# First slab's split in two, rotary remainders after the first evictions, memory scores ahead of the mixer's output, middle sums a tile later

## The chip, the cores and the metric

The kernel runs on one core of one Trainium2 chip. Its time is the device time of one launch in microseconds (us); of several runs the median stands. Engines: PE (TensorE: matmuls and their weight loads), DVE (VectorE), ACT (ScalarE), POOL (GpSimd) and SP, which here only issues transfers. They run side by side and meet at semaphores.

## The reference, cut to what matters

Four transformer layers at float32, on 512 tokens of width 1024. Of the first block:

```python
for l in range(DEPTH):
    h = rms_norm(x, mix_norm[l])
    kv = mem_n @ w_mem_kv[l]
    if kind == 0:
        mixed, mq = attn_mixer(h, positions, attn_w_in[j], attn_sinks[j])   # rotary, windowed heads
    else:
        mixed, mq = lru_mixer(h, lru_w_in[j], ...)        # conv, two gated recurrences, gelu gate
    mo = memory_attention(mq, mk, mv)                     # 4 heads over 256 memory tokens
    x = x + jnp.concatenate([mixed, mo], axis=-1) @ w_out[l]
    x = x + squared_relu_mlp(rms_norm(x, mlp_norm[l]), w_up[l], w_down[l])
return rms_norm(x, final_norm)
```

The second block starts from that normed output and has two layers of gated MLP (silu(h @ wg) * (h @ wu)), neighbourhood attention with gated linear attention, and a second gated MLP; a last rms norm ends it.

## The kernel before

**Layout.** Activations are held transposed: a tile is 128 features by 512 tokens, `x` has eight. Weights come in **slabs** of 128 x 2048 floats (16 blocks of 128 x 128), two buffers deep (`w_raw`, `w_hi`, `w_lo`, slot = slab number modulo 2). SP loads a raw slab when the slab two before it is split (`lo_done`). ACT then writes `w_hi`, the weights rounded to the matmul's type (`split_high`, L1332), and DVE writes the remainder `w_lo` = `w_raw` - `w_hi` (`split_low`, L1732, counted by `lo_done`). Activations are split the same way (`xg_hi`, `xg_lo`; `hid_hi`, `hid_lo`; `mixL_hi`, `mixL_lo`). Each product is three matmuls of 128 x 512: hi by hi, hi by lo, lo by hi, summed in PSUM. Eight feature tiles make 24 matmuls for one output tile, 48 for a slab of two. DVE evicts (`proj`, `tmp`, `x`), multiplying with the reciprocal root of the mean square, `r_bc`; the semaphore `evac` counts evictions, `mm_done` the matmuls of finished blocks.

**Order.** There is no scheduler: each engine's program is written out by hand and runs in that order, and semaphores alone tie them. A late instruction holds up all behind it on its engine.

**The start.** ACT splits `x` tiles 0 to 3, then the first slab as a whole, then tiles 4 to 7 and the second slab; DVE follows with the remainders. PE's first matmul waits for `lo_done` 1, the whole of the first slab. After the first slab PE sums squares over partitions (`token_rms`, L801): it waits for DVE's sum `x_sq` (L2389) and raises `ss_mm`, which releases ACT's root (`r_bc`, L1397) and POOL's squares of the memory (`mem_sq`, L638 and L641). DVE makes the rotary tables' arguments in a chain of small operations, each waiting for the one before: `rope_ang`, then for the sine (n = 0) `rope_k` three times and `rope_r` four times, then the reciprocal of `r_bc` (L1834), the eviction of slab 0 (L1772), the split of slab 2, and the chain again for the cosine (n = 1). PE, one tile into slab 1, turns values (`values()`, L1079), for which both tiles of slab 0 have to be evicted. ACT's sine (L1422) waits for both arguments, and PE's rotary swaps (L1091) for the eviction of slab 1.

**out1_0**, the first output projection (8 slabs of 12 blocks, one output tile each). Its first two slabs are multiplied in pieces inside the attention (`first_out`, L889). DVE and ACT then go slab by slab (`each_slab`): eviction into `x`, ACT `xg_hi` of the new tile, then the split of the slab two on. PE's next slab (L857) waits for that split. POOL sums squares of each new `x` tile (L655 to L661).

**The mixer of layer 1** (`mixer()` on PE, ACT and DVE). Ten slabs come in (`dense(j)` on PE, `inward(j)` on DVE, L2064), and eight recurrences run on DVE beside them (`recur`, `output`, `low`), with tanh, exp and root on ACT. Tiles 16 to 19 of `proj` (slabs 8 and 9) are the memory queries. Then the output projection: `out(h, part, b)`, 12 matmuls each (L1173), h the half of the output tiles, part 0 and 1 the mixer's features, part 2 the memory's. Memory attention has 8 units (`M1`, two heads by 128 queries): PE `scores` (L937), DVE `front` (copy, maximum, negation: L1903, L1906, L1921), ACT `exponentials` (L1431), PE `turn_probs` (L948), ACT `take_turned` (L1442), PE `weigh` (L958), DVE `back` (L1932, L1935), PE `turn_out` (L970), DVE `finish` (L1962, L1964). PE's `turn_out` of a unit waits for `finish` of the one before it. Before: PE does `out(0, 0, 0..3)`, then `scores` of units 0 and 1, then the units' loop with `out(0, 1, b)` in it.

**The middle norm.** The first block's final norm and the second block's first norm are folded together. POOL makes two sums of squares, tile by tile (`two_squares`, L675 to L689), and `token_rms` turns them over partitions with three fp32 matmuls (L804 to L806), after the first output tile of `up2_0_0_0`. Each slab there (swiglu) has two tiles, gate and up; DVE evicts both (L1804), multiplies, splits, and only then follows the split of the slab two on.

## Time and profile before

| | us |
|---|---|
| median of 3 runs | 3400.54 |
| lowest, highest | 3397.35, 3403.29 |
| the profiled execution | 3402.28 |
| its span, first to last instruction | 3400.5 |
| busy in it: PE, DVE, ACT, POOL | 3284.3, 1787.6, 1130.6, 408.6 |

Mean granted TensorE clock of the profiled execution: 0.979. The profile shows one execution; all its times are from the span's start. PE is the engine that is nearly always busy, so what the others do matters where PE waits for it, and there alone. PE's waits are the view to begin with, then the order in time around each.

### The profile page before, as it was taken

How to read it: one execution, taken by the hardware profiler on the slowest of the kernel's cores; microseconds unless marked ns; L12 is line 12 of the kernel's file. 1: busy time of each engine (PE TensorE's matmuls, PEld its weight loads, DVE VectorE, ACT ScalarE, POOL GpSimd, SP SyncE). 2: the span in 40 equal slices, each digit the busy share in tenths (PEclk: the TensorE clock that was granted, in tenths of full speed). 3: DMA queues.
4: the chain of work that ended last, by engine and by line, in shares of the span. 5: the costliest groups of instructions: out<-in, count | busy, mean ns of one | idle time of the engine just before them, and what ended most of it. 6: DMA issues, size and time to landing. Idle time of an engine off the chain costs nothing. (4 is left out here: it accounts for less than half of the span.)

```text
span 3400.5 us, 40741 instructions
## 1 busy us (share of the span) xinstructions
PE 3284.3 (97%) x15310; PEld 2700.3 (79%) x15310; DVE 1787.6 (53%) x1923; ACT 1130.6 (33%) x1314; POOL 408.6 (12%) x319
## 2 busy tenths in 40 slices
PE   7999999999899999999999899999999999799998
PEld 5887888877788887888877688888888878688887
DVE  7764534459553445434556654345444546644344
ACT  3353322259332222322333233223322334333221
POOL 1001100110100033000222420002000211520002
PEclk9999999999999999999999899999999999699999
DMA  3111222222122224232221022324222221022222
GB/s 145 63 52 61 99 99 99 109 96 81 50 99 99 87 98 117 90 108 85 100 75 62 1 87 89 108 85 129 93 102 94 104 75 63 13 74 88 102 90 79
DMA packets 46196, 293.19 MB, mean 86 GB/s; under 512 B 5424, under 2 KB 5936, under 8 KB 17936
## 3 DMA queue, kind: packets, MB, share of 16 engines
q1 hardware_dynamic: 44640, 287.04, 24.0%
q0 software_dynamic: 1456, 4.79, 0.8%
q8 instruction: 67, 1.10, 0.1%
q14 instruction: 33, 0.27, 0.0%
HBM read 289.70 MB, written 2.10 MB: 86 GB/s over the span
## 5 line engine op out<-in xcount | busy, mean ns | idle before, releaser
L1732 DVE TENSOR_TENSOR w_lo<-w_raw,w_hi 128x2048 fp32r<-128x2048 f32 (+1 forms) x288 | 677.6, 2353 | 271.1 <-ACT w_hi L1332 271.1
L857 PE MATMUL ps<-xg_hi,w_hi 128*128 128x512 f32 x1920 | 749.6, 390 | 0.0
L857 PE MATMUL ps<-xg_hi,w_lo 128*128 128x512 f32 x1920 | 747.0, 389 | 0.0
L857 PE MATMUL ps<-xg_lo,w_hi 128*128 128x512 f32 x1920 | 747.0, 389 | 0.0
L1332 ACT ACTIVATE w_hi<-w_raw 128x2048 fp32r<-128x2048 f32 (+1 forms) x288 | 544.9, 1892 | 522.5 <-PE ps L857 357.7
L857 PE MATMUL ps<-hid_hi,w_hi 128*128 128x512 f32 x1216 | 473.3, 389 | 0.0
L857 PE MATMUL ps<-hid_hi,w_lo 128*128 128x512 f32 x1216 | 473.1, 389 | 0.0
L857 PE MATMUL ps<-hid_lo,w_hi 128*128 128x512 f32 x1216 | 473.1, 389 | 0.0
L857 PEld LDWEIGHTS ps<-xg_hi,w_hi 128*128 128x128 f32 x1920 | 360.6, 188 | 76.1 <-issue 1.7
L857 PEld LDWEIGHTS ps<-xg_lo,w_hi 128*128 128x128 f32 x1920 | 360.5, 188 | 76.3 <-issue 1.6
L857 PEld LDWEIGHTS ps<-xg_hi,w_lo 128*128 128x128 f32 x1920 | 360.5, 188 | 74.9
L1817 DVE SCALAR_TENSOR_TENSOR x<-ps,x 128x512 f32 (+1 forms) x120 | 83.0, 692 | 402.1 <-PE ps L857 398.9
L1804 DVE TENSOR_TENSOR tmp<-ps,r_bc 128x512 f32<-128x512 f32 x176 | 121.7, 691 | 322.9 <-PE ps L857 307.2
L857 PEld LDWEIGHTS ps<-hid_hi,w_hi 128*128 128x128 f32 x1216 | 228.3, 188 | 48.5 <-issue 1.4
L857 PEld LDWEIGHTS ps<-hid_lo,w_hi 128*128 128x128 f32 x1216 | 228.3, 188 | 47.4
L857 PEld LDWEIGHTS ps<-hid_hi,w_lo 128*128 128x128 f32 x1216 | 228.3, 188 | 47.2
L655 POOL TENSOR_TENSOR ssq<-x 128x512 f32<-128x512 f32 x9 | 9.4, 1041 | 2047.2 <-DVE x L1817 1849.7
L1375 ACT ACTIVATE hid_hi<-tmp 128x512 f32 x88 | 55.7, 632 | 387.2 <-DVE tmp L1807 387.2
L1385 ACT ACTIVATE xg_hi<-x,vec x64 | 46.3, 724 | 350.0 <-DVE x L1817 350.0
L1000 PE MATMUL ps<-xg_hi,w_hi 128*128 128x512 f32 x384 | 154.2, 402 | 0.0
L1000 PE MATMUL ps<-xg_lo,w_hi 128*128 128x512 f32 x384 | 150.2, 391 | 0.0
L1000 PE MATMUL ps<-xg_hi,w_lo 128*128 128x512 f32 x384 | 150.1, 391 | 0.0
(337 smaller groups left out, 4103.8 us busy)
## 6 DMA issues: line engine op xcount, KB each, us to landing
w_raw<-up_dram SPq DMA_DIRECT2D x120, 1024.0 KB, 4.8
w_raw<-down_dram SPq DMA_DIRECT2D x32, 1024.0 KB, 4.8
w_raw<-down_dram SPq DMA_DIRECT2D x32, 768.0 KB, 4.3
w_raw<-down_dram SPq DMA_DIRECT2D x32, 640.0 KB, 3.8
w_raw<-in_dram SPq DMA_DIRECT2D x18, 1024.0 KB, 4.8
w_raw<-out_dram SPq DMA_DIRECT2D x14, 1024.0 KB, 4.8
w_raw<-in2n_dram SPq DMA_DIRECT2D x12, 1024.0 KB, 4.8
w_raw<-in2g_dram SPq DMA_DIRECT2D x12, 1024.0 KB, 4.8
```

The source lines that it names most:

```text
L655: pool.tensor_tensor(ssq[:], x[:, 0, :], x[:, 0, :], ALU.mult).then_inc(ssq_ready, 1)
L857: last = pe.matmul(to, (w_hi, w_lo)[wp][:, q, t:t + P], parts[xp], start=(k == 0 and m == 0), stop=(k == p.ktiles - 1 and m == 2))
L1000: last = pe.matmul(ps[:, bank, :], (w_hi, w_lo)[wp][:, s % 2, t:t + P], (xg_hi, xg_lo)[xp][:, k, :], start=(k == 0 and m == 0), stop=(k == ...
L1332: act.activation(w_hi[:, q, 0:w], w_raw[:, q, 0:w], ACT.Copy).then_inc(hi_done, 1)
L1375: act.activation(pick(hid_hi, j), tmp[:, 1, :], ACT.Copy).then_inc(hid_h, 1)
L1385: act.activation(pick(xg_hi, m), pick(x, m), ACT.Copy, scale=g).then_inc(xg_h, 1)
L1732: dve.tensor_tensor(w_lo[:, q, 0:w], w_raw[:, q, 0:w], w_hi[:, q, 0:w].bitcast(F32), ALU.subtract)\
L1804: dve.tensor_tensor(tmp[:, b, :], ps[:, 2 * q + b, :], r_bc[:], ALU.mult).then_inc(evac, Q // 2)
L1817: dve.scalar_tensor_tensor(out=pick(x, m), in0=ps[:, bank + b, :], scalar=p.alpha, in1=pick(x, m), op0=ALU.mult, op1=ALU.add).then_inc(eva ...
```

## The change

Same arithmetic, same matmuls, same transfers. Six edits, at five places in time:

1. **Start.** ACT and DVE split the first slab in two halves (one output tile each); new semaphores `first_hi` and `first_lo` tell of the first half. PE waits for `first_lo` before tile 0, for `lo_done` 1 before tile 1.
2. **Rotary chain.** The sine's remainder steps (`rope_r` for n = 0, four operations) move from before the reciprocal to after the eviction of slab 0 and the split of slab 2.
3. **out1_0.** For its first slab ACT and DVE split slab `s0 + 2` ahead of `xg_hi` and `xg_lo`, and 1536 wide instead of 2048. ACT's first iteration is written out instead of looped.
4. **Mixer, order.** PE does `scores` of unit 0 before `out(0, 0, 0)`, and of unit 1 between b = 2 and b = 3. DVE evicts the last slab before `output(6)` instead of after, and does `front` of unit 0 there. ACT's order follows.
5. **Mixer, splits.** The split of slab `MIX_O + 1` goes behind DVE's `output(7)`; that of `MIX_O + 2` from before the units into the loop, behind `back` of unit 1 (on ACT behind `take_turned` of unit 1).
6. **Middle norm.** `token_rms` comes after both tiles of the first slab of `up2_0_0_0` instead of after the first.

```diff
@@ PE, product() @@
-                slab(0, 0, (lambda: token_rms(rms)) if rms is not None else None)
+                if p.norm == MID + 1 and rms is not None:
+                    slab(0, 0)
+                    token_rms(rms)
+                else:
+                    slab(0, 0, (lambda: token_rms(rms)) if rms is not None else None)
                 slab(0, 1)
@@ PE, first_projection() @@
-                pe.wait_ge(lo_done, j + 1)
+                if j:
+                    pe.wait_ge(lo_done, j + 1)
...
                 for b in range(2):
+                    if j == 0:
+                        pe.wait_ge((first_lo, lo_done)[b], 1)
@@ PE, mixer() @@
+            pe.wait_ge(gate_read, DT)
+            pe.wait_ge(evac, EV0 + Q * (MIX_O - 1))
+            scores(M1[0])
             pe.wait_ge(evac, EV0 + Q * MIX_O)
             for b in range(4):
                 out(0, 0, b)
-            pe.wait_ge(gate_read, DT)
-            scores(M1[0])
-            scores(M1[1])
+                if b == 2:
+                    scores(M1[1])
@@ ACT, each_slab() @@
                 for q in range(2):
+                    ahead = p.name == "out1_0" and isinstance(i, int) and i == q == 0
+                    if ahead:
+                        split_high(s0 + 2, 0, p.tiles * P)
                     epilogue(i, q)
-                    if split:
+                    if split and not ahead:
@@ ACT, mixer() @@
             for n in range(DT):
+                if n + 1 == DT:
+                    gelu_square(n)
                 split(MIX_IN + n + 4)
                 if n + 1 < DT:
                     gates(n + 1, True)
                 else:
-                    gelu_square(n)
+                    exponentials(M1[0], 0)
...
-            split(MIX_O + 2)
-            exponentials(M1[0], 0)
             for n, u in enumerate(M1):
                 if n + 1 < len(M1):
                     exponentials(M1[n + 1], n + 1)
                 take_turned(u, n)
+                if n == 1:
+                    split(MIX_O + 2)
@@ ACT, start @@
-            split_high(q, q, SLAB_T * P)
+            if q == 0:
+                act.wait_ge(slab_in[0], 16)
+                for n, done in enumerate((first_hi, hi_done)):
+                    h = slice(DT * P * n, DT * P * (n + 1))
+                    act.activation(w_hi[:, 0, h], w_raw[:, 0, h], ACT.Copy).then_inc(done, 1)
+            else:
+                split_high(q, q, SLAB_T * P)
@@ DVE, resid() @@
                                              op0=ALU.mult, op1=ALU.add).then_inc(evac, Q // p.blocks)
+                if p.name == "out1_0" and isinstance(i, int) and i == q == 0:
+                    split_low(s0 + 2, 0, p.tiles * P)
@@ DVE, first_tables(); before the first eviction only rope_angles() and rope_turns(0) are left @@
             if slab == 0:
-                rope_tables(1)
+                rope_remainder(0)
+                rope_turns(1)
+                rope_remainder(1)
@@ DVE, mixer() @@
-                inward(n + 2)
-                split(MIX_IN + n + 4)
                 if n + 1 < DT:
+                    inward(n + 2)
+                    split(MIX_IN + n + 4)
                     inputs(n + 1)
+                else:
+                    front(M1[0], 0)
...
+                if n + 2 == DT:
+                    inward(DT + 1)
                 output(n)
+            split(MIX_O + 1)
             low(DT - 1)
-            split(MIX_O + 2)
-            front(M1[0], 0)
             front(M1[1], 1)
             for n, u in enumerate(M1):
                 if n + 2 < len(M1):
                     front(M1[n + 2], n + 2)
                 back(u)
+                if n == 1:
+                    split(MIX_O + 2)
                 if n:
                     finish(M1[n - 1])
```

DVE around the first eviction, in the kernel before:

```order
L2001 TENSOR_SCALAR rope_k<-rope_ang 128x512 [waits rope_step]
L2002 TENSOR_SCALAR rope_k<-rope_k 128x512 [waits rope_step]
L2003 TENSOR_SCALAR rope_k<-rope_k 128x512 [waits rope_step]
L2004 SCALAR_TENSOR_TENSOR rope_r<-rope_k,rope_ang 128x512 [waits rope_step]
L2007 SCALAR_TENSOR_TENSOR rope_r<-rope_k,rope_r 128x512 [waits rope_step] x2
L2010 TENSOR_SCALAR rope_r<-rope_r 128x512 [waits rope_step]
L1834 RECIPROCAL r_bc<-r_bc 128x512 [waits ss_rt]
L1772 TENSOR_TENSOR proj<-ps,r_bc 128x512 [waits mm_done,r_ready]
L1772 TENSOR_TENSOR proj<-ps,r_bc 128x512 [waits mm_done]
L1732 TENSOR_TENSOR w_lo<-w_raw,w_hi 128x2048 [waits hi_done]
L2001 TENSOR_SCALAR rope_k<-rope_ang 128x512
```

and with the change:

```order
L2023 TENSOR_SCALAR rope_k<-rope_ang 128x512 [waits rope_step]
L2024 TENSOR_SCALAR rope_k<-rope_k 128x512 [waits rope_step]
L2025 TENSOR_SCALAR rope_k<-rope_k 128x512 [waits rope_step]
L1858 RECIPROCAL r_bc<-r_bc 128x512 [waits ss_rt,rope_step]
L1794 TENSOR_TENSOR proj<-ps,r_bc 128x512 [waits mm_done,r_ready]
L1794 TENSOR_TENSOR proj<-ps,r_bc 128x512 [waits mm_done]
L1754 TENSOR_TENSOR w_lo<-w_raw,w_hi 128x2048 [waits hi_done]
L2033 SCALAR_TENSOR_TENSOR rope_r<-rope_k,rope_ang 128x512
L2036 SCALAR_TENSOR_TENSOR rope_r<-rope_k,rope_r 128x512 [waits rope_step] x2
L2039 TENSOR_SCALAR rope_r<-rope_r 128x512 [waits rope_step]
L2023 TENSOR_SCALAR rope_k<-rope_ang 128x512
```

The four `rope_r` operations now stand behind the reciprocal, the two evictions and the split.

DVE at the end of the mixer's recurrences, before:

```order
L2126 TENSOR_TENSOR l_v<-l_v 128x512 [waits h_done]
L2110 SCALAR_TENSOR_TENSOR l_y<-l_y,proj 128x512 [waits gelu_done]
L2130 SCALAR_TENSOR_TENSOR l_y<-l_y,l_v 128x512 [waits hs_done,gg_done]
L2064 TENSOR_TENSOR proj<-ps,r_bc 128x512 [waits mm_done] x2
L1732 TENSOR_TENSOR w_lo<-w_raw,w_hi 128x2048 [waits hi_done]
L2135 TENSOR_TENSOR mixL_lo<-l_y,mixL_hi 128x512 [waits y_hi]
L2104 SCALAR_TENSOR_TENSOR l_y<-l_y,proj 128x512 [waits gelu_step]
...
L2135 TENSOR_TENSOR mixL_lo<-l_y,mixL_hi 128x512 [waits y_hi]
L1732 TENSOR_TENSOR w_lo<-w_raw,w_hi 128x2048 [waits hi_done]
L1903 TENSOR_SCALAR sc_m<-ps 128x512 [waits s_ready]
L1906 TENSOR_REDUCE mx<-sc_m 128x2 [waits s_read]
L1921 TENSOR_SCALAR nmx<-mx 128x2 [waits mx_done]
```

and with the change:

```order
L2093 TENSOR_TENSOR proj<-ps,r_bc 128x512 [waits mm_done] x2
L2155 TENSOR_TENSOR l_v<-l_v 128x512 [waits h_done]
L2139 SCALAR_TENSOR_TENSOR l_y<-l_y,proj 128x512 [waits gelu_done]
L2159 SCALAR_TENSOR_TENSOR l_y<-l_y,l_v 128x512 [waits hs_done,gg_done]
L1929 TENSOR_SCALAR sc_m<-ps 128x512 [waits s_ready]
L1932 TENSOR_REDUCE mx<-sc_m 128x2 [waits s_read]
L1947 TENSOR_SCALAR nmx<-mx 128x2 [waits mx_done]
L2164 TENSOR_TENSOR mixL_lo<-l_y,mixL_hi 128x512 [waits y_hi]
L2133 SCALAR_TENSOR_TENSOR l_y<-l_y,proj 128x512 [waits gelu_step]
```

The eviction of the last slab (`proj`) and the first unit's scores (`sc_m`) move forward, and the split of `MIX_O + 1` leaves this place. It follows `output(7)`, and the split of `MIX_O + 2` comes to stand in the units' loop, ahead of the first unit's `finish`:

```order
L1947 TENSOR_SCALAR nmx<-mx 128x2 [waits exp_done,mx_done]
L1958 RECIPROCAL rec<-rowsum 128x2 [waits exp_done]
L1961 TENSOR_TENSOR tmp<-ps,rec 128x256 [waits o_psum,rec_done]
L1754 TENSOR_TENSOR w_lo<-w_raw,w_hi 128x2048 [waits hi_done]
L1988 CAST mixM_hi<-ps 128x2x128 [waits ot_psum]
L1990 TENSOR_TENSOR mixM_lo<-ps,mixM_hi 128x2x128 [waits ot_hi]
```

## Rows read from the trace of the kernel before

**Rows 1.** The page, busy us, share of the span and instructions of each engine.
```profile
PE 3284.3 (97%) x15310; PEld 2700.3 (79%) x15310; DVE 1787.6 (53%) x1923; ACT 1130.6 (33%) x1314; POOL 408.6 (12%) x319
```

**Rows 2.** PE's waits: line waiting <- what ended it: us in total, times, longest.
```profile
PE ps L1109 <- DVE w_lo L1732: 14.7, 1, 14.7
PE ps L1079 <- DVE proj L1772: 6.4, 1, 6.4
...
PE ps L937 <- DVE sc_m L1903: 4.1, 1, 4.1
...
PE ps L804 <- POOL tmp L689: 3.6, 1, 3.6
PE ps L1173 <- DVE proj L2064: 3.3, 1, 3.3
PE ps L857 <- DVE w_lo L1732: 3.3, 1, 3.3
```

**Rows 3.** Timeline of DVE from the start: start us, us taken, operation, count, [idle before].
```profile
12.35 2.29 DVE L1732 TENSOR_TENSOR w_lo<-w_raw,w_hi 128x2048 fp32r<-128x2048 f32 x1 [0.90 <-ACT w_hi L1332]
...
20.76 4.35 DVE L2389 TENSOR_TENSOR x_sq<-x_sq 128x2048 f32<-128x2048 f32 x3 [1.27 <-ACT x_sq L1689]
...
26.93 0.43 DVE L2003 TENSOR_SCALAR rope_k<-rope_k 128x512 f32<-128x512 f32 x1
...
28.12 4.70 DVE L2007 SCALAR_TENSOR_TENSOR rope_r<-rope_k,rope_r 128x512 f32<-128x512 f32 x2
32.85 2.47 DVE L2010 TENSOR_SCALAR rope_r<-rope_r 128x512 f32<-128x512 f32 x1
35.24 3.34 DVE L1834 RECIPROCAL r_bc<-r_bc 128x512 f32<-128x512 f32 x1
38.67 1.29 DVE L1772 TENSOR_TENSOR proj<-ps,r_bc 128x512 f32<-128x512 f32 x2
```

**Rows 4.** Timeline of POOL from 25 to 45 us.
```profile
28.30 3.97 POOL L638 TENSOR_TENSOR mem_sq<-mem_raw 128x2048 f32<-128x2048 f32 x1 [27.46 <-PE ps L801]
32.35 4.90 POOL L641 TENSOR_TENSOR mem_sq<-mem_sq 128x1024 f32<-128x1024 f32 x3
```

**Rows 5.** Stretches: us; busy (x) of PE, PEld, DVE, ACT, POOL; PEclk; DMA share, GB/s.
```profile
14.70:17.80 3.10, 3.06 (x7) 2.48 (x8) 3.10 (x5) 3.10 (x5) 0.00 (x0) 1.00 1.06 391
17.80:27.10 9.30, 9.30 (x42) 7.64 (x41) 7.75 (x9) 4.21 (x7) 0.00 (x0) 1.00 0.51 195
38.30:45.10 6.80, 4.99 (x16) 4.34 (x17) 6.54 (x10) 0.00 (x0) 0.00 (x0) 0.50 0.24 73
850.70:857.50 6.80, 5.51 (x13) 4.35 (x14) 5.50 (x7) 4.86 (x5) 0.00 (x0) 0.50 0.09 22
1311.40:1314.90 3.50, 3.50 (x6) 1.35 (x4) 0.00 (x0) 0.00 (x0) 0.00 (x0) 0.51 0.32 136
```

**Rows 6.** Timeline of PE, the token sums and the turned values.
```profile
27.19 1.02 PE L801 MATMUL ps<-x_sq,ones 128*128 128x512 f32 x2
...
40.11 1.94 PE L1079 MATMUL ps<-ident,proj 128*128 128x128 f32 x8 [6.41 <-DVE proj L1772]
```

**Rows 7.** Timeline of POOL and ACT at the first slab of out1_0.
```profile
307.98 1.04 POOL L655 TENSOR_TENSOR ssq<-x 128x512 f32<-128x512 f32 x1 [270.73 <-DVE x L1817]
...
308.70 1.90 ACT L1332 ACTIVATE w_hi<-w_raw 128x2048 fp32r<-128x2048 f32 x1
```

**Rows 8.** The mixer's end: DVE's timeline, then the first weighing on PE's.
```profile
850.65 1.28 DVE L2064 TENSOR_TENSOR proj<-ps,r_bc 128x512 f32<-128x512 f32 x2
...
867.80 2.29 DVE L1732 TENSOR_TENSOR w_lo<-w_raw,w_hi 128x2048 fp32r<-128x2048 f32 x1 [4.12 <-ACT w_hi L1332]
...
872.50 0.69 DVE L1903 TENSOR_SCALAR sc_m<-ps 128x512 f32<-128x512 f32 x1 [0.88 <-PE ps L937]
...
875.77 0.94 PE L958 MATMUL ps<-mv,pt_m 128*128 128x128 f32 x6 [0.61 <-ACT pt_m L1442]
```

**Rows 9.** The stretch 848.7 to 863.7, busy of PE, PEld, DVE, ACT, POOL, as in group 5.
```profile
848.70:863.70 15.00, 11.71 (x40) 9.45 (x41) 12.85 (x16) 7.22 (x8) 0.00 (x0) 0.77 0.19 71
```

More of the change, by code:

```diff
@@ L320, in program @@
     mem_ready = sem("mem_ready")
+    first_hi = sem("first_hi")
+    first_lo = sem("first_lo")
     xg_h = sem("xg_h")
@@ L1711, in _ @@
             else:
-                each_slab(p, epilogue(p))
+                each_slab(p, epilogue(p), 1 if p.name == "out1_0" else 0)
             if p.name == "in1_0":
@@ L1741, in body @@
                     epilogue(i, q)
-                    if split:
+                    if split and not (p.name == "out1_0" and isinstance(i, int) and i == q == 0):
                         split_low(s0 + q + 2, q, w, i, 2)
@@ L1983, in _, with rope_link, rope_angles, rope_turns @@
         rope_n = [0]
-        def rope_tables(n):
-            def link(ins):
-                rope_n[0] += 1
-                ins.then_inc(rope_step, 1)
-                dve.wait_ge(rope_step, rope_n[0])
+        def rope_link(ins):
+            rope_n[0] += 1
+            ins.then_inc(rope_step, 1)
+            dve.wait_ge(rope_step, rope_n[0])
+        def rope_angles():
+            dve.wait_ge(win_in, 48)
+            rope_link(dve.tensor_copy(rope_ang[:], rope_pos[:]))
+            rope_link(dve.tensor_scalar(rope_ang[:], rope_ang[:], v("inv_freq"), None, ALU.mult))
+        def rope_turns(n):
+            big = 1.5 * 2 ** 23
+            rope_link(dve.tensor_scalar(rope_k[:], rope_ang[:], 1 / (2 * math.pi), 0.25 * n, ALU.mult, ALU.add))
+            rope_link(dve.tensor_scalar(rope_k[:], rope_k[:], big, None, ALU.add))
+            rope_link(dve.tensor_scalar(rope_k[:], rope_k[:], -big, None, ALU.add))
+        def rope_remainder(n):
             two_pi = 2 * math.pi
@@ L2385, in _ @@
                     .then_inc(xg_ready, 1)
-            split_low(q, q, SLAB_T * P)
+            if q == 0:
+                for n, (ready, done) in enumerate(((first_hi, first_lo), (hi_done, lo_done))):
+                    h = slice(DT * P * n, DT * P * (n + 1))
+                    dve.wait_ge(ready, 1)
+                    dve.tensor_tensor(w_lo[:, 0, h], w_raw[:, 0, h], w_hi[:, 0, h].bitcast(F32), ALU.subtract)\
+                        .then_inc(done, 1)
+            else:
+                split_low(q, q, SLAB_T * P)
         dve.wait_ge(xsq_done, DT)
@@ L2399, in _ @@
             if p.name == "in1_0":
-                rope_tables(0)
+                rope_angles()
+                rope_turns(0)
             if p.kind == "proj" or (p.kind in ("relu2", "swiglu") and p.group == 0):
```

16 lines of the change are left out of this document (4 added, 12 removed).

## The prediction

> **What bounds the kernel now.** I read the page first: PE is busy for 97% of the span, DVE for 53%, ACT for 33% [rows 1]. So a part of the change is worth what it takes from PE's waits, or from the time PE spends at its low clock. Then PE's waits, which name five places that the diff touches [rows 2]: 14.7 us before the first matmul, 6.4 for the evicted tiles of slab 0, 3.3 for the split in out1_0, 3.3 and 4.1 at the mixer's output, 3.6 for the middle sums. Then the timelines around them and the granted clock. Behind four of the six the clock falls to 0.5, that is 1.2 GHz, for a while after PE has stood still (three are shown: [rows 5]), and what PE does meanwhile takes twice as long. 0.2% of the time, what a measurement can tell from no change, is 6.8 us.
>
> **1. The split start.** DVE is idle for 0.90 us before it splits the first slab at 12.35, so it is free at 11.45 [rows 3], when ACT would have the first half done. Half of 2.29 us, with its fixed part about 1.2, gives 12.7, and PE starts at 12.8 instead of 14.7. That gain is not yet one: PE runs into its token sums (27.19 [rows 6]), which wait for DVE's sum of squares, done at 20.76 + 4.35 = 25.1 [rows 3]; two more instructions on ACT and DVE put that at about 25.2. PE issues seven matmuls in 3.06 us at the start (0.43 each) and then 42 in 9.3 us (0.22, with overlap 0.23) [rows 5]. The faster pace came at 17.8. If it comes at 17.8 again, 5.0 us after PE's first matmul, PE does 12 matmuls slowly and 36 at 0.23, and reaches the token sums at 26.2. I take this: after the restart at 40.1 the clock was back at 45.1, 5.0 us on, and after the one at 852.0 at 857.5, 5.5 us on; only at the start was it 3.1 [rows 5, 6].
>
> **2. The rotary remainders.** Before, DVE's path from the sums to the eviction holds `rope_k` (0.43 each) and four `rope_r`, two of them 4.70 us and the last 2.47 instead of 0.43 [rows 3]. Both long ones end just after an operation of POOL: 28.30 + 3.97 = 32.27, and the next, begun at 32.35 [rows 4]. The reciprocal (3.34) and the eviction ran beside POOL's last operations at their usual length. So DVE operations on SBUF alone with two inputs, or `tensor_scalar`, stand still while POOL reads, and the others do not. The Trainium skill (SBUF — State Buffer, Who interferes with whom) says the same: GpSimd and such VectorE operations share a port pair that one of them holds for a whole instruction. What that rule does here is the first rival.
>
> With token sums at 26.2 POOL asks at 26.2 + 1.1 (28.30 - 27.19) = 27.3 and ACT's root is there at 28.0. The third `rope_k` ends at 26.93 + 0.43 + 0.1 = 27.5, so none of the three is caught. From the start of the reciprocal to the end of the evictions is 38.67 + 1.29 - 35.24 = 4.7 us, so they end at 32.7 instead of 39.96. PE is through its tile at 33.7 - 1.0 = 32.7 (40.11 - 6.41 = 33.7 before [rows 6]) and goes on at 32.9: 7.2 us gained. The low clock from 38.3 to 45.1, with PE busy for 4.99 us, cost 2.5 [rows 5], and goes too.
>
> Late next is DVE. Before slab 1 is evicted it has the split of slab 2 (2.3; POOL's second operation holds it up to about 33.7), four more `rope_r` (2.7, at 0.7 each as in the eviction row, the last 0.4) and the cosine chain (4.4), with POOL's two short operations (1.7) between: 33.7 + 2.3 + 1.7 + 2.7 + 4.4 = 44.8, and 45.9 with the evictions. PE has 0.9 for the turned values and two tiles of 24 x 0.23 = 5.5 and is there at 44.7: a new wait of 1.2. Parts 1 and 2 together: 7.2 + 2.5 - 1.2 = **8.5**. Bounds: 1.7 (rival 1) and 9.7 (no new wait).
>
> **3. out1_0.** Before, `w_hi` starts at 308.70 behind `xg_hi` and takes 1.90 [rows 7], `w_lo` 2.29, and PE starts at about 313.0. Now `w_hi` starts when slab 0 is multiplied, which is one eviction (0.7) and 0.15 before POOL's square of its tile at 307.98 [rows 7], so at 307.1, and is three quarters wide (about 1.45): 308.6. POOL's square of the new tile holds the port from 307.98 to 309.02 [rows 7], so `w_lo` (1.7) ends at 310.7: **2.3** gained. Bounds 1.6 and 2.7.
>
> **4. The mixer.** Before, DVE evicts the last slab from 850.65 to 851.93 [rows 8] behind `output(6)`, though PE was done at 852.0 - 3.3 = 848.7 [rows 2, 8]. Now PE does the first scores in that gap, and begins its output at 850.1. From 848.7 to 863.7 DVE is busy for 12.85 us [rows 9]; in the new order all that stands in one piece, the first `front` (1.6) added, to 863.3. The second `front` follows at once, and from a `front` to the weighing it releases is 875.77 - 872.50 = 3.3 us [rows 8]: the first weighing comes at 866.6 instead of 875.8. In this lies the split of `MIX_O + 2`, which held DVE from 867.80 on [rows 8], and the low clock from 850.7 [rows 5]. PE's own work up to there, 48 matmuls at 0.23, two scores and one set of turns, ends near 864 at full clock. Gained: 9.2. Given back: the moved split stands before `finish` of unit 0, which PE's `turn_out` of unit 1 waits for: one split, 2.2. PE has two new short waits in front of that. Sum **7.0**. Bounds: 9.2 if the split finds a gap, 4.0 if the clock falls in the new waits and costs a further 3 (as 5.51 busy us at 0.50 did [rows 5]).
>
> **5. The middle sums.** PE's 3.6 us wait goes [rows 2]: it does the second tile (5.5) from 1307.1 to 1312.6, when POOL's sums are there: PE was at work on them before 1311.4, since it is busy for all of that stretch [rows 5] (1307.1 is about 1310.7, the start before, less 3.6). The low clock of 1311.4 to 1314.9 [rows 5] goes with it (1.7). The three sums, 0.9 each, end at 1315.3, as before, so the root, the reciprocal (3.34) and the evictions come no later. Late next: root 0.7, reciprocal 3.4, evictions 1.3, product and `hid_hi` 1.5, splits 1.9 and 2.3 put the third slab at 1326.4, and PE is there at 1315.1 + 48 x 0.23 = 1326.0. Sum 3.6 + 1.7 - 0.4 = **4.9**; bounds 3.6 (the clock falls elsewhere) and 5.3.
>
> The two extra DVE and ACT instructions and ACT's unrolled iteration cost PE nothing: both engines wait for PE in all other slabs. No transfer is added or later than its buffer's use.
>
> **Sum.** 8.5 + 2.3 + 7.0 + 4.9 = 22.7 us. The profiled execution took 3402.3, so 3379.6; the median of the runs stands 1.7 below it: **3378**.
>
> **Rival 1: POOL takes the port among the `rope_k`, and edit 2 brings next to nothing.** The clock may rise soon after PE's start, as the 3.1 us before [rows 5] say. Then the token sums come at 25.3, right behind DVE's sum, and POOL asks at 26.4, while the first `rope_k` runs. The second stands still for 4 us, the third for POOL's next operation, 2.2 [rows 4]. The evictions end at 38.0 and only 2.0 us are gained: 3384. If PE is there between 25.4 and 25.9, one `rope_k` is caught alone: 4.1 gained, 3382. By the Trainium skill's rule (SBUF — State Buffer, Who interferes with whom) the one that issues first keeps the other out for its whole length; the 4.70 and 2.47 us of the trace agree. For it: the gap between the cases is 0.5 us of PE's arrival. Against: of the three restarts shown two had the clock back only after 5.0 us or more.
>
> **Rival 2: the mixer gives it back.** The units' loop waits on DVE for each `turn_out`, or the clock falls again: 4.0 instead of 7.0, or less: 3381 to 3385.
>
> **Rival 3: slower, by the clock.** At 0.979 mean clock PE spends about 143 us at 1.2 GHz, most of it in the gated attention of layers 3 and 4, where its waits are short and many. All of that now comes 23 us earlier against whatever sets the clock. It decides from 59 us more at the low level on, 29.5 us lost: with 22.7 gained, that is 3407. The lowest and highest of three runs differ by 6 us, so a shift of that size has not been seen.
>
> **How the numbers follow.** Forecast 0.50; rival 1 0.35; rival 2 0.09; nothing to be measured (several gains lost together) 0.04; rival 3 0.02. The lower bounds add to 10.8, that is 3389.8 by the median; the upper to 26.9, 3373.7; the spread of single runs puts the low end at 3372. Faster 0.94, same 0.04, slower 0.02.
>
> **What would show it.** PE's first matmul at 12.8; PE's wait at the turned values under 1 us and one of about 1 at the rotary swaps (rival 1: 3.5 to 6.5 us at the turned values, and a `rope_k` of 4 us); in out1_0 a `w_lo` of 1536 and a PE wait of 1 us; at the mixer no wait above 2.5 us, the longest at `turn_out` of unit 1; no wait at the middle sums. Wrong would be: a wait at those sums, DVE's `w_lo` or `front` late in the units, or more than 60 us of added low clock.

## The result, and the profile after

The changed kernel takes **3379.72 us**, the median of 5 runs (3377.11 to 3384.31); the kernel before took 3400.54 in the same comparison (3397.35 to 3406.14, now 5 runs too). The ratio is 0.9938 with a 95% interval of 0.9923 to 0.9952, so it is faster by 20.8 us, a little over 0.6%. The forecast was 3378 in a range of 3372 to 3390. The profiled execution of after is the fastest of its five.

| | before | after |
|---|---|---|
| median of the runs, us | 3400.54 | 3379.72 |
| the profiled execution, its time | 3402.28 | 3377.11 |
| its span | 3400.5 | 3375.3 |
| mean granted clock of TensorE | 0.979 | 0.983 |

The page of after, busy us and share of the span, which answers to [rows 1]:
```profile
PE 3274.8 (97%) x15310; PEld 2692.4 (80%) x15310; DVE 1784.5 (53%) x1924; ACT 1130.1 (33%) x1315; POOL 409.2 (12%) x319
```
PE's busy time fell by 9.5 us although it does the same 15310 matmuls: that part of the gain is clock. The rest is waits. PE's waits in after, as in [rows 2]: line waiting, what ended it, us in total, times, longest.
```profile
PE ps L1118 <- DVE w_lo L2424: 12.9, 1, 12.9
...
PE ps L976 <- DVE mixM_lo L1990: 5.1, 6, 2.4
...
PE ps L859 <- DVE w_lo L1754: 1.6, 2, 1.0
...
PE ps L943 <- DVE sc_m L1929: 1.1, 1, 1.1
...
PE ps L1182 <- DVE proj L2093: 0.8, 1, 0.8
...
PE ps L1097 <- DVE proj L1794: 0.4, 1, 0.4
PE ps L1085 <- DVE proj L1794: 0.2, 1, 0.2
```
The 14.7 has become 12.9, the 6.4 for the evicted tiles 0.2, the 3.3 of out1_0 1.0, the 3.3 at the mixer's output 0.8, the 4.1 at the scores 1.1, and the 3.6 at the middle sums has no row any more. New are the longest wait of `mixM_lo` (1.1 before, 2.4 now), 1.4 instead of 0.6 for ACT's `pt_m`, and 0.4 at the rotary swaps. The row of `mixM_lo` before:
```profile
PE ps L970 <- DVE mixM_lo L1964: 3.1, 6, 1.1
```

The start, on DVE, POOL and PE in after (start us, us taken, [idle before]), to set against [rows 3, 4, 6]:
```profile
27.06 0.43 DVE L2025 TENSOR_SCALAR rope_k<-rope_k 128x512 f32<-128x512 f32 x1
28.17 3.35 DVE L1858 RECIPROCAL r_bc<-r_bc 128x512 f32<-128x512 f32 x1 [0.68 <-ACT r_bc L1411]
31.61 1.29 DVE L1794 TENSOR_TENSOR proj<-ps,r_bc 128x512 f32<-128x512 f32 x2
32.82 2.83 DVE L1754 TENSOR_TENSOR w_lo<-w_raw,w_hi 128x2048 fp32r<-128x2048 f32 x1
35.57 1.77 DVE L2033 SCALAR_TENSOR_TENSOR rope_r<-rope_k,rope_ang 128x512 f32<-128x512 f32 x1
```
```profile
27.42 3.60 POOL L640 TENSOR_TENSOR mem_sq<-mem_raw 128x2048 f32<-128x2048 f32 x1 [26.59 <-PE ps L803]
31.10 6.83 POOL L643 TENSOR_TENSOR mem_sq<-mem_sq 128x1024 f32<-128x1024 f32 x3
```
```profile
26.32 1.02 PE L803 MATMUL ps<-x_sq,ones 128*128 128x512 f32 x2
...
45.38 1.10 PE L1097 MATMUL ps<-proj,rope_swap 128*128 128x512 f32 x2 [0.35 <-DVE proj L1794]
```
The third `rope_k` began at 27.06, 0.36 us before POOL asked for the port, so none was held; the reciprocal followed the root, and the evictions ended at 32.90 instead of 39.96. What POOL still holds up (the `w_lo` of slab 2, 2.83 instead of 2.28, and two `rope_r`) lies behind the evictions now.

Stretches of after (us; busy and count of PE, PEld, DVE, ACT, POOL; PEclk; DMA share, GB/s), for [rows 5]:
```profile
38.30:45.10 6.80, 6.72 (x30) 5.25 (x28) 6.49 (x13) 5.20 (x6) 0.00 (x0) 1.00 0.23 99
850.70:857.50 6.80, 4.33 (x27) 3.40 (x26) 4.85 (x10) 3.29 (x11) 0.00 (x0) 1.00 0.44 154
1288.00:1300.00 12.00, 12.00 (x49) 8.88 (x49) 4.40 (x2) 2.55 (x3) 4.79 (x3) 1.00 0.35 113
```
The low clock behind the first evictions is gone, in the mixer too, and PE is busy without a pause through the middle sums (1288 to 1300).

**Where the 25 us came from.** I set the same instruction of both traces side by side at four points, and the end of the span: PE's window scores in front of which it waits for DVE's `sc_first` ("first scores" from here on), its first own slab of out1_0, the first matmul of the mixer's `out(0, 2, 0)`, and the first gathering of values in the gated attention. Before, then after:
```profile
129.03 0.59 PE L937 MATMUL ps<-proj 64*128 64x384 f32 x1 [0.89 <-DVE sc_first L1897]
313.06 0.49 PE L857 MATMUL ps<-mixA_hi,w_hi 128*128 128x512 f32 x1 [3.31 <-DVE w_lo L1732]
908.81 0.50 PE L1173 MATMUL ps<-mixM_hi,w_hi 128*128 128x512 f32 x1 [0.97 <-DVE mixM_lo L1964]
1724.04 0.44 PE L1015 MATMUL ps<-ident,vgat 128*128 128x128 f32 x2 [2.97 <-POOL vgat L722]
```
```profile
120.13 0.59 PE L943 MATMUL ps<-proj 64*128 64x384 f32 x1 [0.89 <-DVE sc_first L1923]
301.84 0.49 PE L859 MATMUL ps<-mixA_hi,w_hi 128*128 128x512 f32 x1 [1.02 <-DVE w_lo L1754]
890.29 0.50 PE L1182 MATMUL ps<-mixM_hi,w_hi 128*128 128x512 f32 x1 [0.97 <-DVE mixM_lo L1990]
1700.89 0.69 PE L1021 MATMUL ps<-ident,vgat 128*128 128x128 f32 x2 [2.95 <-POOL vgat L724]
```

| point | before | after | ahead by | so this part gave | predicted |
|---|---|---|---|---|---|
| first scores | 129.03 | 120.13 | 8.90 | parts 1 and 2: 8.9 | 8.5 |
| out1_0, first slab | 313.06 | 301.84 | 11.22 | part 3: 2.3 | 2.3 |
| mixer, (0, 2) | 908.81 | 890.29 | 18.52 | part 4: 7.3 | 7.0 |
| first gathering | 1724.04 | 1700.89 | 23.15 | part 5: 4.6 | 4.9 |
| end of the span | 3400.5 | 3375.3 | 25.2 | no edit lies here: 2.0 | 0 |

The edits carry 23.15 of the 25.2. The last 2 us come where nothing was changed. The next sections show that the first line of the table can come out at 2 to 9 us.

### The profile page after: what moved, and what is told of

Its sections match the earlier page's. It is cut to its first block and busy times, and to the rows that moved or that the text cites. A ratio compares the mean times of both kernels' runs of the same rounds, so it can differ in the third digit from the quotient of the medians.

```text
span 3375.3 us, 40736 instructions
## 1 busy us (share of the span) xinstructions
PE 3274.8 (97%) x15310; PEld 2692.4 (80%) x15310; DVE 1784.5 (53%) x1924; ACT 1130.1 (33%) x1315; POOL 409.2 (12%) x319
## 5 line engine op out<-in xcount | busy, mean ns | idle before, releaser
L1399 ACT ACTIVATE xg_hi<-x,vec (+1 forms) x64 | 46.3, 724 | 334.7 <-DVE x L1839 334.7
```

What stands on the lines that cost most here:

```text
L1399: act.activation(pick(xg_hi, m), pick(x, m), ACT.Copy, scale=g).then_inc(xg_h, 1)
```

## The experiments

The total of one run spreads over 6 us and more, so the single runs are read at the points above, not by their totals.

When PE's clock "rises" is read from where the trace's record of the granted clock begins. Before that moment the stretches show a PEclk of 1.00 ([rows 5], 14.70 to 17.80), but PE starts a matmul of 512 columns every 0.43 us there, and every 0.23 us after it: 1.2 and then 2.4 GHz.

**start_alone**: the kernel before with edit 1 only.
```diff
-            split_high(q, q, SLAB_T * P)
+            if q == 0:
+                act.wait_ge(slab_in[0], 16)
...
```


> The kernel before with the split start alone (slab 0 of the weights split by tiles, PE waits per tile); the rotary remainders, out1_0, mixer and sums as before. Theory (POOL and DVE share a port, and an earlier start only moves PE's token sums to another place among DVE's rotary operations): PE starts at 12.8, POOL asks for the port at about 27.4, and finds the four rope_r operations in front of the reciprocal, of which three are caught instead of two and a half; the evictions of slab 0 end at about 41.6 instead of 39.96, so PE goes on at the turned values at 41.7, 1.6 us LATER than before (40.11). The start alone brings nothing. Rival (the two edits add up, each its own gain): the evictions end 1.9 to 2 us earlier than before, at about 38. Told by PE's wait and start at the turned values, and the length of each rope_r; the total of one run is not read (its spread is 6 us).

PE started at 12.60. POOL asked at 26.64, earlier than the 27.4 expected, and caught the last `rope_k` and three `rope_r`, DVE:
```profile
26.81 3.71 DVE L2014 TENSOR_SCALAR rope_k<-rope_k 128x512 f32<-128x512 f32 x1
30.55 2.76 DVE L2015 SCALAR_TENSOR_TENSOR rope_r<-rope_k,rope_ang 128x512 f32<-128x512 f32 x1
33.35 2.76 DVE L2018 SCALAR_TENSOR_TENSOR rope_r<-rope_k,rope_r 128x512 f32<-128x512 f32 x2
```
```profile
41.35 0.45 PE L1081 MATMUL ps<-ident,proj 128*128 128x128 f32 x1 [9.32 <-DVE proj L1783]
```
PE went on 1.24 us later than before [rows 6], and at the first scores it stood at 129.19 against 129.03. The split start alone brings nothing: PE's 2.1 us turn into a wait of 9.32 in place of 6.41. The additive rival falls.

**rotary_alone**: the kernel before with edit 2 only.
```diff
             if slab == 0:
-                rope_tables(1)
+                rope_remainder(0)
+                rope_turns(1)
+                rope_remainder(1)
```


> The kernel before with the rotary remainders moved behind the first evictions alone; PE starts at 14.7 as before. Theory (the port): the reciprocal starts at about 29.0, straight behind the root, the evictions end at 33.7, PE's own tile at 33.7, so PE goes on at about 33.9 instead of 40.11, without a low clock behind; at the rotary swaps it is 8 us ahead of before. So this edit alone carries 8.0 of the 8.9 us that both bring, and the start adds about 1 on top of it. Rival (additive): it brings 8.9 - 1.9 = 7.0 or less, because the start's own 1.9 us is missing at every later point.

PE went on at 34.95, not 33.9, and the first scores came at 122.05: 7.0 gained, not 8.0. The mechanism was as expected (no DVE operation in front of the reciprocal held up, no low clock behind), but in this execution PE's clock rose only at 19.95, 5.2 us after its first matmul, where it had risen after 3.1 in the trace of before [rows 5]; the token sums came 1.0 us later for it (28.23 against 27.19). By the first scores alone this run can't be told from the additive rival; start_alone tells them apart. So 0 and 7.0 alone make 8.9 together.

**warm_pe**: the changed kernel with 48 matmuls of constants before PE's first weight tile.
```diff
         pe.wait_ge(setup, 3)
+        for _ in range(48):
+            pe.matmul(ps[:, 7, 0:P], ones[:], ones[:], start=True, stop=True)
```


> The changed kernel with 48 further matmuls of the constant ones into an unused bank of PSUM before PE's first weight tile arrives, so that the clock should be at full speed when the first real matmul starts at 12.8. This makes rival 1 of the prediction happen. Theory (one of POOL and DVE holds the port pair for a whole instruction): token sums at about 25.3 instead of 26.3, POOL asks at about 26.4 while the first rope_k runs, the second rope_k stands still until POOL's first square ends (about 4 us), the third until the next (about 2.3), the evictions end at about 38 and PE goes on there some 5 us LATER than in the changed kernel (33.05), although PE did its first tiles sooner. Rival (operations of one input and a scalar like rope_k are not held up; only the rope_r with two tensor inputs are): the rope_k keep 0.43 us each, the evictions end at about 32.1, bound by DVE's own chain.

The 48 matmuls lasted until 14.25, so PE's first real matmul came at 14.01, later than the 12.8 meant. But the clock was at full speed from there on: the token sums came at 25.22, POOL asked at 26.43, and two `rope_k` were caught:
```profile
26.52 3.80 DVE L2026 TENSOR_SCALAR rope_k<-rope_k 128x512 f32<-128x512 f32 x1
30.35 2.49 DVE L2027 TENSOR_SCALAR rope_k<-rope_k 128x512 f32<-128x512 f32 x1
32.88 3.35 DVE L1860 RECIPROCAL r_bc<-r_bc 128x512 f32<-128x512 f32 x1
```
PE waited 5.93 us for the evictions and went on at 37.75, 4.7 us later than in the changed kernel; the first scores stood at 126.87, only 2.2 ahead of before. PE at full clock costs 6.7 us here. This is rival 1 of the prediction, made to happen, to within 0.2 us of its price (2.0). Operations with one input and a scalar are held up as those with two are; the reciprocal (3.35), with POOL at work until 34.76, is not.

**warm_pe_late_pool**: the same, and POOL's first square waits for the evictions of slab 0.
```diff
         pool.wait_ge(mem_in, 16)
+        pool.wait_ge(evac, EV0 + Q)
```


> As the kernel with the warm PE, and POOL's first square of the memory inputs also waits until the evictions of slab 0 are done, so that POOL is away from the port while DVE does its rope_k and the reciprocal. Theory (the port): no rope_k is longer than 0.43 us, the evictions end at about 32.2 and PE goes on at the turned values at about 32.4, 0.6 us before the changed kernel; 5 us or more before the kernel with the warm PE alone. Rival (it is PE's earlier activity or its own order that delays DVE): no difference between this and the warm PE alone.

No `rope_k` was held, and PE went on at 33.20 after a wait of 0.50 (DVE's own sum of squares was 0.9 us later here, for a reason that the run does not show; that explains 33.20 instead of 32.4). But all of POOL's squares now meet the `rope_r` behind the evictions:
```profile
35.17 4.09 DVE L2036 SCALAR_TENSOR_TENSOR rope_r<-rope_k,rope_ang 128x512 f32<-128x512 f32 x1
39.30 4.48 DVE L2039 SCALAR_TENSOR_TENSOR rope_r<-rope_k,rope_r 128x512 f32<-128x512 f32 x2
```
```profile
50.36 1.19 PE L1098 MATMUL ps<-proj,rope_swap 128*128 128x512 f32 x1 [5.18 <-DVE proj L1797]
```
The wait is 5.18 us at the swaps instead of 0.35, and the first scores came at 127.16, worse than with the warm PE alone. The port's cost was moved, not removed, and I had not counted what stood behind the gate.

**The start, seven times.** The kernels below that leave the start as the change made it give, with after and after_again, seven executions of the same code there. Times in us; "held" are the `rope_k` that POOL kept waiting:

| execution | first matmul | clock rises | POOL asks | third `rope_k` starts | held | PE's wait | first scores |
|---|---|---|---|---|---|---|---|
| after | 12.85 | 18.11 | 27.42 | 27.06 | none | 0.2 | 120.13 |
| mixer_undone | 13.01 | 18.62 | 27.75 | 27.21 | none | 0.2 | 120.48 |
| after_again | 12.66 | 17.28 | 26.94 | 26.87 | none | 0.2 | 119.88 |
| split_ahead | 12.94 | 17.37 | 27.12 | 27.15 | third | 3.40 | 122.44 |
| split_in_gap | 12.65 | 16.82 | 26.68 | 26.86 | third | 3.40 | 122.00 |
| sums_undone | 12.76 | 15.91 | 26.43 | 30.34 | second, third | 5.93 | 126.85 |
| out_wide | 12.66 | 16.16 | 26.38 | 30.30 | second, third | 5.92 | 126.91 |

One instruction decides. In after_again POOL came 0.07 us after the third `rope_k` had begun, in split_ahead 0.03 us ahead of it:
```profile
26.94 3.81 POOL L640 TENSOR_TENSOR mem_sq<-mem_raw 128x2048 f32<-128x2048 f32 x1 [26.11 <-PE ps L803]
```
```profile
27.15 3.86 DVE L2024 TENSOR_SCALAR rope_k<-rope_k 128x512 f32<-128x512 f32 x1
31.04 3.35 DVE L1857 RECIPROCAL r_bc<-r_bc 128x512 f32<-128x512 f32 x1
```
Whoever asks first has the port: POOL's square is 0.21 longer where `rope_k` was first, `rope_k` 3.43 longer where POOL was. In sums_undone, with two held, the clock fell behind PE's wait of 5.93:
```profile
36.40:43.20 6.80, 5.46 (x17) 4.71 (x18) 6.63 (x10) 0.00 (x0) 0.00 (x0) 0.50 0.31 99
```
So parts 1 and 2 gain 8.9, 8.6 or 9.2 in three executions, 6.6 and 7.0 in two, 2.2 and 2.1 in two: 6.4 on the mean, against the one profiled execution of before. This mean is over executions of seven runs whose kernels differ later on, not over seven of one kernel.

Set beside it rotary_alone, which gained 7.0 by itself, with a late rise of the clock. POOL asked there at 29.33, 1.9 us after the third `rope_k` had ended, and in before, where the clock rose earliest of all, at 28.30, 0.9 us after it. So with the late start no execution on record comes near the race. As far as one execution of rotary_alone can tell, the earlier start (edit 1) adds nothing on the mean to edit 2, and it is what makes its gain uncertain.

**mixer_undone**: the changed kernel with the mixer's order (both parts of it, scores and split) as before.
```diff
-            pe.wait_ge(gate_read, DT)
-            pe.wait_ge(evac, EV0 + Q * (MIX_O - 1))
-            scores(M1[0])
             pe.wait_ge(evac, EV0 + Q * MIX_O)
             for b in range(4):
                 out(0, 0, b)
-                if b == 2:
-                    scores(M1[1])
+            pe.wait_ge(gate_read, DT)
+            scores(M1[0])
+            scores(M1[1])
```


> The changed kernel with the order of the mixer's output as it was before (scores behind the output, first front and ACT's exponentials behind the split of MIX_O + 2); all other parts of the change stay. Theory: at the output of unit (0, 2), the last point of the mixer, it stands 11.2 us ahead of the kernel before (what parts 1 to 3 bring, as at the last dense), instead of 18.5; so the mixer's part is worth 7.3 us, the waits of 3.3 and 4.1 us at PE and the low clock behind them are back. Rival (part of the gain at the mixer came from elsewhere, a changed phase of the clock): it stands 13 us or more ahead.

The waits are back (3.64 at the output, 4.12 at the scores), and (0, 2) stood at 896.02, 12.8 us ahead of before: more than 11.2, less than the rival's 13. From the end of the last dense to (0, 2) it took 59.44 us against 52.86 in after and 60.14 in before. The mixer's part is 6.6 to 7.3; the 0.7 between them is clock, which was low for about 6.8 us in this stretch here and for 10.2 in before. The rest of what it is ahead by is clock too, in the attention of the window (low for 6.8 us from 165.4 on, where it was 10.2 in after).

**split_ahead**: the changed kernel with the split of `MIX_O + 2` in front of the units again, on ACT and DVE.
```diff
             low(DT - 1)
+            split(MIX_O + 2)
             front(M1[1], 1)
...
-                if n == 1:
-                    split(MIX_O + 2)
```


> The changed kernel with the split of MIX_O + 2 back in front of the units, on ACT and DVE, before the second front; scores and first front stay early. Theory: DVE's and ACT's path to the first weighing is longer by one split, the weighing comes 2.3 to 3.4 us later (855.24 in the changed kernel's own time), the wait of 2.4 us at the turned output of unit 1 goes, so at (0, 2) it stands 1 to 1.5 us behind the changed kernel, and the scores ahead carry 6 of the 7.3 us, the moved split the rest. Rival (the moved split is what pays; the scores only moved the wait): 5 us or more behind the changed kernel.

```profile
857.31 2.07 PE L943 MATMUL ps<-mk,proj 128*128 128x256 f32 x4 [4.55 <-DVE sc_m L1928]
859.84 1.44 PE L964 MATMUL ps<-mv,pt_m 128*128 128x128 f32 x5 [0.46 <-ACT pt_m L1456]
```
```profile
857.10:863.90 6.80, 6.13 (x20) 4.96 (x21) 3.05 (x8) 3.26 (x10) 0.00 (x0) 0.50 0.43 154
```
From the first output matmul to (0, 2) it took 54.46 us instead of 51.19: 3.3 lost. In waits alone the split's place is nearly even: 3.48 more at the scores, 0.94 less at the weighing, 2.37 less at the turned output, 0.17 in all. The loss is the clock, which fell behind the one long wait: 6.13 busy us at 1.2 GHz, some 3.1 too many. So neither the theory's 1 to 1.5 nor the rival's 5: the moved split pays by cutting one wait of 4.6 into three of 1.1, 1.4 and 2.4. Against after_again, where the clock was low for 3.4 us behind those three (52.78), it pays only 1.7.

**split_in_gap**: DVE's split one place earlier than in the changed kernel.
```diff
-                back(u)
                 if n == 1:
                     split(MIX_O + 2)
+                back(u)
```


> The changed kernel with DVE's split of MIX_O + 2 one place earlier, before back of unit 1 instead of behind it, where DVE stands idle for 2.2 us. Theory (DVE's path, with the split in it, is what PE waits for at the turned output of unit 1): the wait of 2.37 us there goes or falls below 0.5, and all behind it comes 1.8 to 2.2 us sooner; PE at (0, 2) 20.5 us ahead of the kernel before instead of 18.5. Rival (DVE is not idle for long enough, or the split then holds up the back of unit 1): the wait moves to another place of the units' loop and 0.5 us or less is gained.

```profile
861.64 2.29 DVE L1754 TENSOR_TENSOR w_lo<-w_raw,w_hi 128x2048 fp32r<-128x2048 f32 x1
...
864.84 0.43 DVE L1990 TENSOR_TENSOR mixM_lo<-ps,mixM_hi 128x256 fp32r<-128x256 f32 x1
```
```profile
865.41 0.41 PE L976 MATMUL ps<-ident,tmp 128*128 128x128 f32 x2 [0.17 <-DVE mixM_lo L1990]
```
The wait fell from 2.37 to 0.17. From the first output to (0, 2) it took 50.68 us with a low clock of 3.4 us in it; the changed kernel took 51.19 without one and 52.78 with one (after_again). Like for like 2.1 gained. The forecast's "2.2 given back" was there to be had.

**sums_undone**: the changed kernel with the middle sums between the two tiles again.
```diff
-                if p.norm == MID + 1 and rms is not None:
+                if False:
```


> The changed kernel with the middle sums of the first half's layer where they were, between the two tiles of the slab. Theory: PE waits 3.6 us for POOL's sums again and the clock falls to 1.2 GHz behind it, in all 4.6 to 4.9 us lost between the end of the mixer and the next gathering of values (18.5 us ahead of before at both, instead of 18.5 and 23.15). Rival (the move only hides the wait and the same is given back at the third slab in any order): less than 3 us lost.

```profile
1300.44 2.05 PE L806 MATMUL ps<-tmp,ones 128*128 128x512 f32 x2 [3.57 <-POOL tmp L691]
```
```profile
1299.40:1306.10 6.70, 5.66 (x7) 2.52 (x8) 0.00 (x0) 0.16 (x1) 0.90 (x1) 0.50 0.35 138
```
From (0, 2) to the first gathering it took 816.39 us, against 810.60 in after and 815.23 in before: 5.8 lost here, more than the 4.6 to 4.9 expected, and 4.6 in before, where the same wait of 3.6 left the clock low for 3.4 us instead of 6.8. The rival (given back at the third slab) falls: that wait is 0.57 in after.

**out_wide**: the early split of out1_0 with all 2048 columns.
```diff
-                        split_high(s0 + 2, 0, p.tiles * P)
+                        split_high(s0 + 2, 0, w)
```


> The changed kernel with the split that stands ahead of the first eviction of out1_0 as wide as in the kernel before (2048 columns instead of 1536). Theory: w_hi takes 1.90 instead of 1.49 and w_lo 2.3 instead of about 1.8, so PE's wait for that w_lo is 0.9 longer than the 1.02 of the changed kernel, about 1.9; two fifths of the 2.3 us come from the narrower split, the rest from the place ahead of the eviction. Rival (POOL's square, which holds the port until 300.09 in the changed kernel, sets when w_lo can start, so that a wider w_hi is hidden by it): only w_lo's own growth counts, 0.3 to 0.5 longer.

ACT and POOL ended within 0.04 us of each other (304.28 + 1.92 and 305.12 + 1.04), and DVE followed:
```profile
306.23 2.29 DVE L1754 TENSOR_TENSOR w_lo<-w_raw,w_hi 128x2048 fp32r<-128x2048 f32 x1 [1.25 <-ACT w_hi L1343]
```
```profile
308.66 0.49 PE L859 MATMUL ps<-mixA_hi,w_hi 128*128 128x512 f32 x1 [1.76 <-DVE w_lo L1754]
```
PE waited 1.76 instead of 1.02: 0.74, between theory (0.9) and rival (0.3 to 0.5). Both are at work: in after the narrow `w_hi` is done at 299.69, and POOL's square, until 300.08, takes part of that back in the `w_lo` (1.98 for 1536 columns).
```profile
299.72 1.98 DVE L1754 TENSOR_TENSOR w_lo<-w_raw,w_hi 128x1536 fp32r<-128x1536 f32 x1 [0.82 <-ACT w_hi L1343]
```

**after_again**: the changed kernel, unchanged, in one comparison with the next version.

> The changed kernel once more, for the version meant to beat it to be set against, and as a further draw of its start. Theory (the start goes three ways): the profiled execution has one of three patterns, by how long after PE's first matmul (12.6 to 13.0) the clock rises: 5.2 us or more, no rope_k caught, first scores at 120.1 to 120.5; 4.1 to 4.5, one caught, 122.0 to 122.5; 3.1 to 3.3, two caught, 126.9. Rival (the patterns belong to the kernels they were seen in, not to chance): 120.1 again.

3381.41 us, the median of 5 (3378.08 to 3383.21), ratio 0.9949 to before (0.9936 to 0.9963). The start is in the table: none held, though the clock rose after 4.6 us, between the bands I had written down. The time from PE's first matmul to the rise of the clock is not the criterion; whether POOL asks before the third `rope_k` is. The rival of this run, that each pattern belongs to its kernel, is not excluded: both executions of the changed kernel itself had none held. What speaks for chance is that between these two POOL's asking moved by 0.48 us and its distance behind the start of the third `rope_k` shrank from 0.36 to 0.07.

**rotary_behind**: a version without the gamble. All of the sine's rotary operations stand behind the evictions of slab 0, the cosine's behind those of slab 1, and the split of `MIX_O + 2` is in its gap.
```diff
             if slab == 0:
+                rope_angles()
+                rope_turns(0)
                 rope_remainder(0)
+            if slab == 1:
                 rope_turns(1)
                 rope_remainder(1)
...
-            if p.name == "in1_0":
-                rope_angles()
-                rope_turns(0)
```


> A version meant to beat both: the changed kernel with DVE's split of MIX_O + 2 in its gap (before back of unit 1), with all of the sine's rotary operations (angles, rope_k, remainders) behind the evictions of slab 0, and the cosine's behind those of slab 1. So DVE has nothing in front of the reciprocal that POOL's squares can hold up, whenever PE reaches its token sums. Theory (the start of the changed kernel goes three ways by the moment at which PE's clock rises: first scores at about 120.3 with no rope_k caught, 122.2 with one, 126.9 with two): here the first scores come at 119 to 120.2 whatever the clock does, PE waits under 0.5 us for the evictions, none at the rotary swaps of slab 0's end, since 2.2 us come into DVE's path there and 4.4 leave it; with 1.7 us more at the mixer, the median lies 3 to 6 us below the changed kernel's of the same call, at a ratio to it of about 0.9985. Rival (DVE's later rotary operations hold up the rotation of slab 2, which PE waits for): a wait of 2 us or more at the rotary swaps of slab 3 (PE at 58 us) and no better than the changed kernel.

**3374.23 us**, the median of 5 (3371.88 to 3377.56), ratio to before 0.9932 (0.9918 to 0.9945), with the runs of before shared with after_again. Against the changed kernel it is 7.2 us less; no interval was taken between the two, but the slowest of its five runs is faster than the fastest of the other's. That is more than the 3 to 6 expected. DVE has nothing to hold up ahead of the reciprocal:
```profile
28.05 3.35 DVE L1858 RECIPROCAL r_bc<-r_bc 128x512 f32<-128x512 f32 x1 [2.63 <-ACT r_bc L1411]
31.49 1.29 DVE L1794 TENSOR_TENSOR proj<-ps,r_bc 128x512 f32<-128x512 f32 x2
```
```profile
44.77 0.59 PE L1097 MATMUL ps<-proj,rope_swap 128*128 128x512 f32 x1
```
The swaps at 44.77 follow without a wait, and so do those of slab 3, so the rival falls. The first scores came at 119.46; output to (0, 2) took 49.03 us, 2.2 less than in after. Against the profile of after this makes 2.8 us, against the means of the seven starts (122.67) and of the six executions with the mixer unchanged (52.29) 6.5; the 7.2 between the medians fits the second better. It has two edits in it, and no run has the rotary one alone.

**rotary_behind_warm**: the same behind the 48 matmuls.

> The version meant to beat both with the 48 matmuls that warm PE in front. Theory: unlike the warmed changed kernel, which lost 6.7 us at the first scores to two caught rope_k, it loses nothing: evictions of slab 0 end at about 32.0, first scores at 119 or just below. Rival (the early token sums hurt by another way than the port, through POOL's squares on the reciprocal or the evictions): the reciprocal is longer than 3.4 us or the evictions end after 34.

PE's first real matmul came at 13.73, the evictions ended at 31.56 and the first scores came at 118.22, the earliest of all. The early clock that cost the changed kernel 6.7 us gains 1.2 here. The reciprocal took 3.35 beside POOL's square.

## Why the prediction came out right, and what was luck in it

- **Parts 1 and 2, predicted 8.5, measured 8.9.** PE's start 12.8 (12.85), the rise of the clock 17.8 (18.1), the token sums 26.2 (26.3), POOL 27.3 (27.4), the end of the evictions 32.7 (32.9): each step holds, and the low clock behind them is gone. The new wait at the swaps was mis-sized, 1.2 forecast and 0.35 measured: I let POOL hold DVE for 2.7 us there (1.0 at the split and 1.7 among the `rope_r`), and it was 2.05 (0.55, and 1.08 and 0.42). The rest of the 0.85 is that PE itself came to the swaps at 45.03, not 44.7.
- **But this is the best of three cases**, and it held in 3 of 7 executions. If these seven stand for the changed kernel, rival 1, which had 0.35, should have had about as much as the forecast. It was not excluded by the profiled run; it was not drawn in it. Its price with two `rope_k` held was right (2.0 forecast, 2.1 and 2.2 measured). With one held it was mis-sized: 4.1 forecast, 6.6 and 7.0 measured. That price left out that the 2.5 us of low clock go: behind a wait of 3.40 the clock stayed up, behind 5.9 it fell. The criterion that I gave, PE's arrival between 25.4 and 25.9, was too coarse as well: DVE's own chain shifts by 0.3 us between executions, so that token sums at 25.84 went free and at 26.02 were caught.
- **The sum by medians.** The edits gave 23.15 in the profiled execution, and 2.0 more fell to it in the gated attention. The medians differ by 20.8 and not by 25.2 because the profiled execution of before lies 1.7 above its median and that of after 2.6 below. With the mean of the starts, 6.4 in place of 8.9, the edits come to 20.6. That this meets the 20.8 shows little: it averages one part alone. Part 4 is 1.1 less on the mean too, part 3 can be more (both below), and how often the kernel before gets a better or worse start was not tried: it has one profile. So the forecast of 3378 is right within the spread of the runs, and in part by luck.
- **Part 3, predicted 2.3, measured 2.3.** `w_hi` of 1536 columns took 1.49 (1.45 forecast), and POOL's square ended 0.4 after it. As forecast, it then set the `w_lo`, which took 1.98 (1.7 forecast). Overlooked: behind the same wait of 3.31, start_alone and rotary_alone had a low clock of 3.4 us, and before had none. From out1_0's first slab to the end of the last dense it took 537.2 and 537.0 us there, and 535.6 in before and wherever the split was moved. So where the clock falls, this part is worth 1.4 to 1.6 more.
- **Part 4, predicted 7.0, measured 7.3.** Both terms, the gain and what is given back, were found: the first weighing came 20.5 us sooner than before with 11.2 brought along, so 9.3 gained (9.2 forecast), and the wait at the turned output of unit 1 is 2.37 where 2.2 was forecast to be given back; split_in_gap takes it away. Part 4 without a low clock in the units is again the luck of the profiled execution: in after_again, sums_undone, warm_pe and out_wide it was low there for 3.4 us, at a price of 1.6 to 1.7. Over the six executions with the mixer as changed the mean is 1.1 above that of after.
- **Part 5, predicted 4.9, measured 4.6.** The wait of 3.6 and the low clock are gone; 0.6 of wait at the third slab was forecast as 0.4. In every kernel with this edit the stretch from (0, 2) to the gathering took 810.6 us, and 815.2 in before, start_alone and rotary_alone.
- **Rival 2** (the mixer gives it back) did not happen. **Rival 3**, slower by the clock, did not either.
- **Slips of the sum.** The lower bounds add to 10.9, not 10.8; the bound of 1.7 for rival 1 is its price of 2.0 elsewhere; PE's 1315.1 + 48 x 0.23 is 1326.1. None moves the forecast by more than 0.1.

The Trainium skill (SBUF — State Buffer, Who interferes with whom) says that issue order decides who blocks. The seven starts agree, with 0.21 us lost by POOL and 3.43 by DVE for a difference of 0.1 us in the asking.

## What to carry to other kernels

When two engines ask for a shared port within a few tenths of a microsecond of each other, a single profile shows one outcome of several: price each, look whether the order is forced by a wait, and prefer the order in which nothing on the path can be held. Gating the second engine only helps if what stands behind the gate can spare the time. And before a wait is shortened ask what PE runs into next: an earlier start (start_alone) or a PE at full clock (warm_pe) is worth nothing, or less, if it makes another engine ask at a worse moment.

## What the runs showed of the hardware that I had not expected

- The time from PE's first matmul to the rise of its clock from 1.2 to 2.4 GHz differed between executions of the same code: 3.1 to 5.6 us over the seven starts. What follows from it in this kernel is up to 7 us at the first scores, 0.2% of the time.
- The length of a wait alone does not say whether the clock falls. It fell at waits of 9.32, 5.93, 4.55, 3.64 (mixer_undone) and 3.57 us (sums_undone), and at the mixer's output at 3.32 (before) and 3.31 (start_alone, rotary_alone). It stayed up behind 3.40 at the start (split_ahead, split_in_gap). In out1_0 a wait of 3.31 had a low clock at it in start_alone and rotary_alone and none in before.
- In the mixer's units, with waits of 1.1, 1.4 and then 2.4 us, the same code had a low clock of 3.4 us in four executions and none in after and warm_pe_late_pool. In three of the four it fell before the wait of 2.4, behind waits no longer than 1.4.
- Between the first and the second gathering of the gated attention, which no kernel here changes, the time ran from 1035.3 to 1040.0 us over all profiled executions. Up to 4.7 us of it are in every total, which is why the experiments were read at points. Their cause is open: the low clock in that stretch summed to 37.5 to 47.8 us, but it was 37.5 in sums_undone with 1037.7 us and 41.0 in mixer_undone with 1035.3.
